# Gate products written to SBUF instead of back to PSUM, and each bank given back after its first reader, in a two-layer diffusion trunk

## The reference

```python
(aq, ak, av, bq, bi, bff, bfb, bg, cq, ck, cv, gts) = jnp.split(h @ p['w_in'][l], COL_SPLITS, axis=-1)
...
ya = oa.reshape(b_, t_, WIDTH_A) @ p['w_branch_a'][l]     # differential attention
yb = obr.reshape(b_, t_, WIDTH_B) @ p['w_branch_b'][l]    # bidirectional recurrence
yc = oc.reshape(b_, t_, WIDTH_C) @ p['w_branch_c'][l]     # grouped-query attention
g = jax.nn.sigmoid(gts.reshape(b_, t_, N_BRANCH, D_MODEL))
merged = g[:, :, 0] * ya + g[:, :, 1] * yb + g[:, :, 2] * yc
out = merged @ p['w_out'][l]
```

## Time and profile before

| | |
|---|---|
| median of 3 runs | 2232.06 us |
| profiled execution, its own time | 2232.06 us |
| its span in the trace | 2230.3 us |
| TensorE matmul busy | 2144.7 us, 96% |
| VectorE busy | 900.3 us, 40% |
| ScalarE busy | 903.4 us, 41% |
| GpSimd busy | 1240.9 us, 56% |
| mean granted TensorE clock | 0.989 of full |

### The profile page before, as it was taken

One profiled execution on the slowest core, in us unless ns is written; L12 is line 12 of the kernel. 1 busy time (PEld: TensorE's weight loads), 2 busy tenths in 40 slices (PEclk: granted clock), 3 DMA queues, 4 the chain that ended last, 5 costly groups with the idle time before them and its releaser, 6 DMA issues.

```text
span 2230.3 us, 32145 instructions
## 1 busy us (share of the span) xinstructions
PE 2144.7 (96%) x13209; PEld 2023.4 (91%) x13209; DVE 900.3 (40%) x1490; ACT 903.4 (41%) x1269; POOL 1240.9 (56%) x972
## 2 busy tenths in 40 slices
PE   6999999999899999999999999999998999899998
PEld 4999997988899898999979999799888999799997
DVE  5122116446755465121251221534576554621123
ACT  3222323246766444323243232324566646423231
POOL 2666553444478464666646666354434955366662
PEclk8999999999999999999999999999999999999998
DMA  7555675433223283445554446552222235244431
GB/s 282 158 164 170 225 234 165 124 88 96 67 77 95 87 319 114 126 139 170 190 182 129 133 125 238 194 151 85 87 81 67 87 116 180 72 133 124 127 123 61
DMA packets 306921, 311.37 MB, mean 140 GB/s; under 512 B 9923, under 2 KB 285655, under 8 KB 306775
## 3 DMA queue, kind: packets, MB, share of 16 engines
q1 hardware_dynamic: 299671, 303.55, 43.3%
q10 hardware_dynamic: 7104, 5.77, 0.8%
HBM read 305.35 MB, written 3.93 MB: 139 GB/s over the span
## 4 chain that ended last, share of the span: by engine, by line
PE 78%; DVE 9%; ACT 6%; POOL 4%; issue 2%; DMA 1%; SPq 0%; DVEq 0%; ACTq 0%
PE X L587 57%; PE S L587 9%; PE Ab L587 5%; POOL w_lo L524 2%; PE S L704 1%; POOL dec L552 1%; POOL dec L551 1%; PE X L765 1%; PE S L794 1%; ACT p L1172 1%; ACT w_hi L1019 1%; DVE y L1557 1%; DVE root L1554 1%; DVE x L1559 1%; DVE root L1532 1%
## 5 line engine op out<-in xcount | busy, mean ns | idle before, releaser
L524 POOL TENSOR_TENSOR w_lo<-raw,w_hi 128x512 fp32r<-128x512 f32 (+1 forms) x872 | 1164.0, 1358 | 939.3 <-ACT w_hi L1019 929.2
L1019 ACT ACTIVATE w_hi<-raw 128x1024 fp32r<-128x1024 f32 (+1 forms) x436 | 452.9, 1041 | 720.6 <-PE X L587 686.6
L587 PE MATMUL X<-h_hi,w_hi 128*128 128x384 f32 x1600 | 538.9, 337 | 13.9 <-DVE h_lo L1512 13.9
L587 PE MATMUL X<-h_lo,w_hi 128*128 128x384 f32 x1600 | 536.0, 335 | 0.0
L587 PE MATMUL X<-h_hi,w_lo 128*128 128x384 f32 x1600 | 535.9, 335 | 0.0
L587 PEld LDWEIGHTS X<-h_hi,w_hi 128*128 128x128 f32 x1600 | 301.2, 188 | 25.9 <-DVE h_lo L1512 17.2
L587 PEld LDWEIGHTS X<-h_lo,w_hi 128*128 128x128 f32 x1600 | 301.3, 188 | 0.0
L587 PEld LDWEIGHTS X<-h_hi,w_lo 128*128 128x128 f32 x1600 | 301.3, 188 | 0.0
L1568 DVE TENSOR_TENSOR prod<-X,silu 128x768 f32<-128x768 f32 x44 | 42.1, 957 | 565.0 <-PE X L587 565.0
L587 PE MATMUL X<-act_hi,w_hi 128*128 128x384 f32 x704 | 236.4, 336 | 0.0
L587 PE MATMUL X<-act_hi,w_lo 128*128 128x384 f32 x704 | 235.3, 334 | 0.0
(11 more groups left out here) (362 smaller groups left out, 3065.3 us busy)
## 6 DMA issues: line engine op xcount, KB each, us to landing
raw<-in_w_in SPq DMA_DIRECT2D x124, 512.0 KB, 3.8
raw<-in_ffn_gate SPq DMA_DIRECT2D x88, 512.0 KB, 3.7
raw<-in_ffn_up SPq DMA_DIRECT2D x88, 512.0 KB, 3.7
raw<-in_ffn_down SPq DMA_DIRECT2D x80, 512.0 KB, 3.5
raw<-in_ada_w SPq DMA_DIRECT2D x48, 512.0 KB, 4.0
hold<-in_ada_w SPq DMA_DIRECT2D x29, 512.0 KB, 5.4
first_w<-in_ada_w SPq DMA_DIRECT2D x16, 512.0 KB, 10.4
hold_a<-in_ada_w SPq DMA_DIRECT2D x16, 512.0 KB, 6.7
```

Of the source, the lines that this page charges most:

```text
L524: ins = nc.gpsimd.tensor_tensor(slot(w_lo, u)[:, part], raw_of(u)[:, part], slot(w_hi, u)[:, part], SUB)
L587: mm = nc.tensor.matmul(dst, w[:, k, m * 128:m * 128 + 128], r_, start=start and k + j == 0, stop=stop and k == u.nk - 1 and j == 2)
L1019: A(slot(w_hi, u), raw_of(u), ACT.Copy).then_inc(hi_ready[u.split], 1)
```

## The change

Both pairs of VectorE instructions are rewritten in the same way. The product of bank and gate goes to the gate's place in SBUF, not back to the bank, and gives the bank free at once. The sum then reads two SBUF tensors; before, it read the bank and one SBUF tensor. In `merge()` the wait on each sum before the following `low` falls away with the separate increment that freed the bank, and so do the eight waits ahead of the loop, replaced by one wait on `gate_free`. The number of VectorE's arithmetic instructions stays what it was.

```diff
@@ fill(), branch c
-                                V.tensor_tensor(G[BANK[g]][:, 0:T], G[BANK[g]][:, 0:T], gates[:, t % 4, :], MUL) \
-                                    .then_inc(S["gate_free"], 1)
-                                dve.wait_ge(S["gate_free"], 8 * L + t + 1)
-                                V.tensor_tensor(acc(t), acc(t), G[BANK[g]][:, 0:T], ADD).then_inc(g_free[BANK[g]], 1)
+                                V.tensor_tensor(gates[:, t % 4, :], G[BANK[g]][:, 0:T], gates[:, t % 4, :], MUL) \
+                                    .then_inc(g_free[BANK[g]], 1)
+                                dve.wait_ge(g_free[BANK[g]], TURN[g] + 1)
+                                V.tensor_tensor(acc(t), acc(t), gates[:, t % 4, :], ADD).then_inc(S["gate_free"], 1)
@@ merge()
-                for t in range(KT):
-
-                    g = TILE_OF[L, "yc", t]
-                    dve.wait_ge(g_free[BANK[g]], TURN[g] + 1)
+                dve.wait_ge(S["gate_free"], 8 * L + 8)
                 for u in PHASES[L, "merge"]:
                     for m in range(2):
                         t, g = 2 * u.tag[1] + m, u.dest + m
                         tile_wait(u, m)
-                        step(V.tensor_tensor(G[BANK[g]][:, 0:T], G[BANK[g]][:, 0:T], gate_b[:, t, :], MUL))
-                        V.tensor_tensor(gate_b[:, t, :], acc(t), G[BANK[g]][:, 0:T], ADD).then_inc(S["sum_made"], 1)
-                        dve.wait_ge(S["sum_made"], 8 * L + t + 1)
-                        dve.sem_inc(g_free[BANK[g]], 1)
+                        V.tensor_tensor(gate_b[:, t, :], G[BANK[g]][:, 0:T], gate_b[:, t, :], MUL) \
+                            .then_inc(g_free[BANK[g]], 1)
+                        dve.wait_ge(g_free[BANK[g]], TURN[g] + 1)
+                        V.tensor_tensor(gate_b[:, t, :], gate_b[:, t, :], acc(t), ADD).then_inc(S["sum_made"], 1)
                         if t:
                             low(t - 1)
                 low(KT - 1)
```

## The result

The changed kernel takes 2254.52 us (median of 4, 2253.01 to 2255.67) against 2231.98 for the kernel before in the same session: 22.5 us or 1.0% slower, the ratio 1.0100 with a 95% interval of 1.0083 to 1.0117. The direction was forecast, the size was not: 7.8 us, at most 11.

A forecast was written before the change was run, and what follows sets the result against it. TensorE, busy 96% of the span, was taken to bound the kernel. Merge 2.0, tiles 6 and 7 1.0 and tiles 0 to 3 0.9 us per layer made 7.8 us, 2239.8 us; 8-in-10 range 2235 to 2243.

The forecast's parts named there:

- What bounds: Whole kernel: TensorE is busy 96% of the span, so VectorE's edits matter only where TensorE waits for VectorE.
- the products: Branch b and c products writing SBUF, not PSUM: 547 ns against 559 each, costed at nothing.
- the sums undisturbed: Sums of two SBUF tensors beside an idle GpSimd: 554 ns as with PSUM, so nothing gained.
- Merge: In merge(): sums and lows wait for GpSimd's port, so TensorE's second w_out unit starts 2.0 us later per layer.
- Tiles 6 and 7: Branch c, before the copy k_bn: both sums meet GpSimd, so k_bn starts 1.0 us later per layer.
- Tiles 0 to 3: Branch c, at the decay levels: sums wait for GpSimd and delay lev_q, costing TensorE 0.9 us per layer.
- TensorE's clock: Rival: the new stall in each merge also lowers TensorE's granted clock, 2 x 1.45 us more, 2242.7 us; chance 0.10.
- The sum: Whole kernel: 2.0 + 1.0 + 0.9 = 3.9 us per layer, 7.8 for two, giving 2239.8 us.
- the signs of being wrong: L1452 stays at 554 ns beside busy GpSimd; VectorE keeps the port twice running; or stalls also cost TensorE's clock.

The follow-up runs named there:

- The merge alone: Kernel before with the changed form only in merge(), branch c in the old form; 2240.84 us against 2232.02, ratio 1.0039.
- branch c alone: Kernel before with the changed form only in branch c's tiles, merge() in the old form; 2244.68 us, ratio 1.0056.
- the levels put back: Changed kernel with tiles 0 to 3 of branch c, at the decay levels, in the old form; 2240.58 us, ratio 1.0040.
- the pause: Changed kernel with one wait added on GpSimd, so it stands idle just before the sum of tile 0; 2241.1 us.
- the sum asks later: Changed kernel with one more VectorE instruction, touching only PSUM, before the product of tile 0; 2253.05 us.

## Why the prediction was wrong

*What bounds, the products, the sums undisturbed.* Right. The products are at 548 ns, sums beside an idle GpSimd at 0.56 us, and nobody gained from the earlier return of a bank.

*Merge.* Right in mechanism and in the size of the wait: +1.9 us per layer against 2.0. The merge alone confirms the wait; its time, 8.8 us for both layers against 4.0, was more than forecast.

*Tiles 6 and 7.* Right: both sums about 1.05 us, k_bn's wait 3.36 against 2.36.

*Tiles 0 to 3: the step that failed.* The prediction took it that the two engines "take turns", so that a sum waits "until GpSimd's current instruction ends", and gave the sum of tile 0 0.2 us. It took 4.3 us more than undisturbed. All rows behind that rule came from GpSimd runs that had just begun (726.40 after a pause of 2.86 us, the merge's pairs after 0.3 to 1.5); at the levels the run was 53 us old, and the kernel before has no VectorE instruction with two SBUF inputs in that run. The term was 0.9 us per layer and measured 3.1 in waits (6.2 / 2). With a pause the rule holds again at this place (0.89 us for the sum), but even then not the 0.9 us: lev_q's wait is 10.6 us, against 11.7 before.

The lock itself is as the Trainium skill has it, "SBUF — State Buffer", "SBUF: two separate sides": the loser is blocked outright and nothing is shared. The 4.87 us sum did its 0.4 us of work only after GpSimd had stopped.

*TensorE's clock: the other term that failed, and the larger one.* The sum put it at nothing. It was listed as a rival at 2.9 us and 0.10; it came, at 8.3 us of matmul busy time. It was set apart from the stalls although showed a dip behind a stall of 2.4 us, and the reason given, that a stall of 2.0 us standing alone would bring none, did not hold in the changed kernel. Matmul busy time rose, in one profiled execution each, by 1.3 us with the merge alone, 1.5 with branch c alone, 3.1 with the levels put back and 3.1 with the pause; by 8.3 in the changed kernel and 8.4 where the sum asks later. The two last are the only ones with both the stand of tile 0 and the merge's wait. Why the two together lose more than each alone, and what decides on a given dip, is left open.

*The sum.* 3.9 us per layer forecast; 6.35 of waits (12.7 / 2) and 4.15 of clock measured. Of the 13.7 us of span beyond the forecast, 8.3 are clock and 4.4 the levels; a wait of 0.7 for k_st that was not forecast is most of the rest. The direction was right for the reason given. Of the signs of being wrong that the prediction lists, the last came: the stalls are there and cost clock as well. That VectorE might be kept out for several GpSimd instructions was not among them.

## What to carry to other kernels

Where VectorE and GpSimd work side by side, count the SBUF inputs of each VectorE instruction on the path: one PSUM operand kept it out of GpSimd's way in every row here, and trading it for SBUF to free a bank nobody waits for cost 1%. Look not only at which GpSimd instruction is under way but at how long GpSimd has run without a pause. And join small two-input instructions into one, since each has to get the port anew: beside a busy GpSimd four of 128x256 took 4.63 us and one of 128x1024 took 1.21 when it asked at a boundary.

## What the runs showed of the hardware that was not expected

A VectorE instruction with two SBUF inputs was let in at GpSimd's next boundary when GpSimd had run unbroken for up to 10.3 us (0.55 and 0.75 us for 128x384), and was shut out until GpSimd stopped at 17.8 us and more (5.55, 7.21, 4.87, 4.29 us). Nothing between 10.3 and 17.8 us was tried, and time and number of GpSimd's instructions were not told apart. A pause of 0.80 us on GpSimd brought the turns back. Why, these runs don't say.
